# Value pages in two sets of buffers, three orders changed in one attention layer of a decoder step

## The chip, the cores and the metric

One core of one Trainium2 chip runs the whole program in one launch. The metric is the device time of one execution in microseconds (us); lower is better. The kernel before has a median of 2101.49 us over 3 runs (2100.57 to 2105.2).

## The reference

One inference step of a two-layer decoder trunk in float32. 512 prompt tokens and 8 sample tokens (one for each of 8 sequences) go through the same weights. Each layer is a half-step SwiGLU feed-forward, a mixer, a second feed-forward and a gated per-layer embedding, with a norm before and after each. Layer 0's mixer is attention with forget gates beside a gated short convolution; layer 1's is a linear recurrence. The change lies in layer 0's mixer alone:

```
q, k, v, f_lin, b_gate, c_gate, x_in = split(h @ w_in)
logf = log_sigmoid(f_lin + b_f)
# prompt: 8 heads of 64, 512 tokens, blocks of 128 queries
s = q @ k.T * scale + cumsum(logf)[q] - cumsum(logf)[k]; causal mask
y_a = softmax(s) @ v
# sample: 8 sequences, each 256 past rows in 2 pages of 128 rows, plus the new row
k_past, v_past, f_past = cache_k[page_table], cache_v[page_table], cache_logf[page_table]
y_a = softmax(q @ [k_past, k].T * scale + decays) @ [v_past, v]
# both
y_b = b_gate * causal_dwconv(c_gate * x_in)
y = concat(y_a, y_b) @ w_out
```

Keys, values, gates and states come out as further outputs.

## The kernel before

Activations lie feature-major: 128 features on the partitions, 520 tokens (512 + 8) along the row, in 8 chunks of features. Each float32 matrix product is made of three products of reduced precision: high part of the weights by high part of the activations, low by high, high by low. A unit of weights (128 x 2048, 1 MB) is loaded by SP into a slot `raw` (three slots), ScalarE copies out the high part `w_hi` (L690), and VectorE writes the low part `w_lo` over the raw one (L1085). Both are called by `done(name)` at a place that the plan (`make_plan`, `refills`) fixes: the name of a tile stands for the unit that is split there, two units ahead of its use. SP issues the load of a unit when the tile three units earlier is finished.

TensorE takes its work in an order written out by hand, and each engine has its own list; semaphores tie them. `acc_ready` counts finished tiles of TensorE, and `drained` (one count for each of the four PSUM accumulators) counts the emptied ones. `claim` makes TensorE wait until an accumulator is empty.

In `attention` a loop over the 8 heads h runs on TensorE (from L2153): column tiles of the projections (`c`, `x` for heads 0 to 3, `b` for heads 4 to 7, each of 8 chunks of 6 products), `transposes(h)` of the probabilities `sc` into two accumulators (L2133), `scores(h + 1)` (L2095), then the values product `pv` of head h (from L2169). At head 7 the transposes stand inside tile `b3`, after one of its chunks, and `scores` falls away. ScalarE (from L889) copies the transposed probabilities into `pt` in two parts, `pt.0` (key blocks 0 and 1) and `pt.2` (2 and 3), takes the exponentials of head h + 1 (L883), copies out the result of the values product into `q` (L916, L917), and then splits the next unit's high part, where this head has one (heads 0, 1, 2, 3, 5 and 6). VectorE (from L1593) drains the column tiles with `scaled` (L1335), runs the softmax of head h + 1 (L1503 to L1518) and then `w_lo`.

The sample tokens' pages are gathered by GpSimd (`gather`, L590): four pages (`RING`) of 256 KB into the one buffer `ring`, first four steps of keys, then four of values, in an order written into its loop over the heads (from L637), among the rows of decays (`decay_row`) and the copies of q and k to the other partitions (`swap_halves`). A gather waits for the TensorE job that used the ring last. TensorE's products with the keys and values (`key_scores` L2022, `decode_out` L2042) have 2 columns each and stand between chunks of the column tiles: `decode_out(0)` in `x3`, 1 to 3 in `b0`, `b1`, `b2`. `xsum`, `ysum`, `rs_post` and the upper right blocks of `sc` hold nothing that is used between the start of this mixer and its output product.

Of the kernel before, what the change touches and what calls it, by code (L numbers as in the profile page):

```python
# [297 lines left out]
def trunk(nc, weights, params_d, const_d, x_d, p_d, kpages_d, vpages_d, lfpages_d, table_d,  # L298
# [8 lines left out]
    with ctx:  # L307
# [3 lines left out]
        def sem(name):  # L311
            return ctx.enter_context(nc.semaphore(name))
# [115 lines left out]

        def outer(ap, b0=0):

            return ap.rearrange("p (b n) -> p b n", n=P)[:, b0::QB - 1, :]
# [18 lines left out]
        ring_loaded = sem("ring_loaded")  # L450
        lf_loaded = sem("lf_loaded")
# [114 lines left out]
        def _(pool):  # L566
# [12 lines left out]
            for s in range(SUBS):  # L579
# [4 lines left out]
                if s == S_AB:  # L584
# [5 lines left out]
                    def gather(step):  # L590

                        src = kpages_d if step < STEPS else vpages_d
                        at = step % STEPS * RING
                        pages = [pool.value_load(table[0:1, n:n + 1], min_val=0, max_val=kpages_d.shape[0] - 1)
                                 for n in range(at, at + RING)]
                        if step:
                            wait_job(pool, f"{s}.dec_{'so'[(step - 1) // STEPS]}{(step - 1) % STEPS}")
                        for i, page in enumerate(pages):
                            pool.dma_start(ring[:, i, :], src[bass.ds(page, 1), :, :]
                                           .rearrange("a p n -> (a p) n")).then_inc(ring_loaded, 16)  # L600

# [35 lines left out]
                    for h in range(2, HEADS):  # L637
# [7 lines left out]
                        if h != 4:  # L645
                            gather(h + 1 if h < 4 else h)
# [23 lines left out]
        def _(act):  # L670
# [189 lines left out]
            def attention(s):  # L860
# [28 lines left out]
                for h in range(HEADS):  # L889
# [13 lines left out]
                    if h + 1 < HEADS:  # L903
                        exponentials(h + 1)
# [13 lines left out]
                    for n in tiles_at(s, h):  # L918
                        done(n)
# [859 lines left out]
        def _(pe):  # L1779
# [229 lines left out]
            def attention(s):  # L2009
# [32 lines left out]
                def decode_out(i, part):  # L2042

                    if part == 0:
                        claim(J[f"{s}.dec_o{i}"])
                        wait_drained(pe, f"{s}.dec_p")
                        pe.wait_ge(ring_loaded, 16 * RING * (STEPS + i + 1))
# [3 lines left out]
                    for c in range(part % 2 * 2, part % 2 * 2 + 2):  # L2051
                        at = (r // PAGES * AC + c) * 2
                        for g in range(PAGES):
                            src = g * BH + b * HEADS + 2 * c
                            ins = nc.tensor.matmul(a[:, 0, at:at + 2], ring[:, r + g, c * P:(c + 1) * P],  # L2055
# [97 lines left out]
                for h in range(HEADS):  # L2153
# [8 lines left out]
                    for m in B_TILES.get(h, []):  # L2162
                        column_tile(f"b{m}", f"b{m // 2 * 2}", m % 2, with_values(h - 3) if h < MIX_HEAD else
                                    lambda c: transposes(MIX_HEAD) if c == 5 else None)
# [6 lines left out]
                    wait_drained(pe, f"{s}.pt{h}.2")  # L2171
# [3 lines left out]
                    for kb in range(QB):  # L2175
                        values = v_tok[:, kb, h * HD:(h + 1) * HD]
                        if kb < QB - 1:
# [136 lines left out]
```

## Time and profile before

| | |
|---|---|
| median of 3 runs | 2101.49 us (2100.57 to 2105.2) |
| profiled execution | 2097.6 us, of which 2095.9 us span |
| TensorE busy (products) | 2073.0 us (99%) |
| weight loads of TensorE | 2050.4 us (98%) |
| VectorE | 1127.0 us (54%) |
| ScalarE | 703.8 us (34%) |
| mean granted clock of TensorE | 0.997 |

The span is from the first to the last instruction of one execution; the profiled execution is longer by 1.7 us that lie around it. Busy times are shares of the span. PE is TensorE's products, PEld its weight loads, DVE VectorE, ACT ScalarE, POOL GpSimd and SP the engine that issues the weights. The granted clock is a share of the full one: 1.00 is 2.4 GHz, and near 0.5 is 1.2 GHz.

### The profile page before, as it was taken

Reading aid. Unit: us, or ns where it says so; the run is one execution under the profiler, and the core shown is the slowest. Engines: PE = TensorE matmul, PEld = TensorE weight load, DVE = VectorE, ACT = ScalarE, POOL = GpSimd, SP = SyncE. Lnnn points to the kernel's source line nnn. Section 1 sums busy time; section 2 is a strip of 40 time slices with the busy share of each in tenths; the row PEclk is TensorE's granted clock in tenths of the full one; section 3 lists DMA queues with packets and bytes.
Section 4 is the critical chain, followed back from the end, with each engine's and each line's share of the span. In section 5 each row is a group of like instructions: output and inputs, shape, how many; then the busy total and the mean of one; then the engine's idle time right before and its main releaser. Section 6 shows DMA issues by size and latency. Waiting matters only on the chain.

```text
span 2095.9 us, 37938 instructions
## 1 busy us (share of the span) xinstructions
PE 2073.0 (99%) x17092; PEld 2050.4 (98%) x17092; DVE 1127.0 (54%) x1509; ACT 703.8 (34%) x877; POOL 46.5 (2%) x93
## 2 busy tenths in 40 slices
PE   8999999999999999999999999999999999999999
PEld 8999999999889999999999999999999999999998
DVE  6443244856767544234686443244898854323467
ACT  5221123423344422122344221122487432212243
POOL 0000000021210000000000000000000000000000
PEclk9999999999999999999999999999999999999999
DMA  5222222145331322222222222222222222222222
GB/s 175 88 92 88 96 101 81 63 152 142 126 128 61 104 98 91 91 101 81 100 75 101 99 91 94 98 82 81 82 100 84 81 101 101 82 100 83 99 92 82
DMA packets 35075, 202.81 MB, mean 97 GB/s; under 512 B 5056, under 2 KB 5344, under 8 KB 16992
## 3 DMA queue, kind: packets, MB, share of 16 engines
q1 hardware_dynamic: 29520, 183.87, 24.9%
q0 software_dynamic: 5392, 16.50, 2.5%
q8 instruction: 135, 2.21, 0.4%
q14 instruction: 28, 0.23, 0.0%
HBM read 193.78 MB, written 4.48 MB: 95 GB/s over the span
## 4 chain that ended last, share of the span: by engine, by line
PE 86%; DVE 10%; ACT 2%; DMA 2%; issue 1%; DVEq 0%; POOLq 0%; POOL 0%; ACTq 0%
PE acc L1790 70%; PE acc L1900 10%; DVE w_lo L1085 2%; PE acc L1831 1%; DVE t L1198 1%; DMA raw<-in_weights 1%; DVE x L1205 1%; DVE act_lo L1211 1%; DVE rs_post L1193 1%; PE acc L1980 1%; PE acc L2034 1%; DVE xsum L1220 1%; PE acc L2055 1%; DVE rs_pre L1193 0%; PE acc L2104 0%
## 5 line engine op out<-in xcount | busy, mean ns | idle before, releaser
L1790 PE MATMUL acc<-act_hi,w_hi 128*128 128x260 f32 x3072 | 622.1, 284 | 0.0
L1790 PE MATMUL acc<-act_hi,w_lo 128*128 128x260 f32 x3072 | 618.0, 283 | 0.0
L1790 PE MATMUL acc<-act_lo,w_hi 128*128 128x260 f32 x3072 | 617.7, 283 | 0.0
L1790 PEld LDWEIGHTS acc<-act_hi,w_hi 128*128 128x128 f32 x3072 | 472.9, 188 | 2.7 <-issue 2.0
L1790 PEld LDWEIGHTS acc<-act_hi,w_lo 128*128 128x128 f32 x3072 | 472.9, 188 | 0.4
L1790 PEld LDWEIGHTS acc<-act_lo,w_hi 128*128 128x128 f32 x3072 | 472.4, 188 | 0.5
L690 ACT ACTIVATE w_hi<-raw 128x2048 fp32r<-128x2048 f32 (+3 forms) x179 | 323.0, 1805 | 298.2 <-DMA raw<-in_weights 298.0
L1085 DVE TENSOR_TENSOR w_lo<-raw,w_hi 128x2048 fp32r<-128x2048 f32 (+3 forms) x179 | 386.6, 2160 | 38.2 <-ACT w_hi L690 38.1
L1335 DVE TENSOR_TENSOR gu<-acc,rs_pre 128x520 f32<-128x520 f32 x164 | 114.5, 699 | 440.6 <-PE acc L1790 440.4
L816 ACT ACTIVATE hid_hi<-gu 128x520 fp32r<-128x520 f32 x86 | 55.0, 639 | 476.4 <-DVE gu L1355 476.4
L1790 PE MATMUL acc<-hid_hi,w_hi 128*128 128x260 f32 x1024 | 206.3, 283 | 0.2
L1790 PE MATMUL acc<-hid_hi,w_lo 128*128 128x260 f32 x1024 | 206.1, 283 | 0.0
L1790 PE MATMUL acc<-hid_lo,w_hi 128*128 128x260 f32 x1024 | 205.7, 282 | 0.0
L1790 PEld LDWEIGHTS acc<-hid_hi,w_hi 128*128 128x128 f32 x1024 | 157.7, 188 | 1.0 <-DVE hid_lo L1358 1.0
L1790 PEld LDWEIGHTS acc<-hid_lo,w_hi 128*128 128x128 f32 x1024 | 157.7, 188 | 0.0
L1790 PEld LDWEIGHTS acc<-hid_hi,w_lo 128*128 128x128 f32 x1024 | 157.7, 188 | 0.0
L1900 PE MATMUL acc<-act_lo,w_hi 128*128 128x260 f32 x696 | 142.2, 286 | 3.7 <-DVE act_lo L1211 3.6
L1423 DVE COPY y<-acc 128x520 f32<-128x520 f32 x32 | 22.4, 700 | 228.7 <-PE acc L1790 228.7
L1900 PE MATMUL acc<-act_hi,w_hi 128*128 128x260 f32 x696 | 144.0, 288 | 0.0
L1900 PE MATMUL acc<-act_hi,w_lo 128*128 128x260 f32 x696 | 140.1, 283 | 0.0
L812 ACT ACTIVATE gu<-gu 128x520 f32<-128x520 f32 x86 | 54.9, 638 | 217.2 <-DVE gu L1335 217.2
L1900 PEld LDWEIGHTS acc<-act_lo,w_hi 128*128 128x128 f32 x696 | 107.0, 188 | 7.6 <-DVE act_lo L1211 7.3
(295 smaller groups left out, 2139.8 us busy)
## 6 DMA issues: line engine op xcount, KB each, us to landing
raw<-in_weights SPq DMA_DIRECT2D x138, 1024.0 KB, 4.8
raw<-in_weights SPq DMA_DIRECT2D x32, 896.0 KB, 4.5
ring<-in_k_pages POOLq DMA_DIRECT2D x16, 256.0 KB, 4.0
ring<-in_v_pages POOLq DMA_DIRECT2D x16, 256.0 KB, 3.7
raw<-in_weights SPq DMA_DIRECT2D x12, 256.0 KB, 5.2
x<-in_x SPq DMA_DIRECT2D x8, 260.0 KB, 6.5
out_y<-x SPq DMA_DIRECT2D x8, 260.0 KB, 2.5
ckb<-ch_rows POOLq DMA_DIRECT2D x8, 256.0 KB, 4.3
```

The source lines that it names most:

```text
L690: nc.scalar.activation(w_hi[n % SLOTS][:, at:size], raw(n, size)[:, at:size], ACT.Copy)\
L812: nc.scalar.activation(g, g, ACT.Silu).then_inc(silu_ready, 1)
L816: nc.scalar.activation(hid_hi[:, j if j < HID[0] else j - HID[0], :], up, ACT.Copy).then_inc(hidh_ready, 1)
L1085: nc.vector.tensor_tensor(w_lo[n % SLOTS][:, at:size], raw(n, size)[:, at:size], w_hi[n % SLOTS][:, at:size].bitcast(F32), ALU.subtract).t ...
L1193: nc.vector.reciprocal(cols(rs, half), cols(rs, half)).then_inc(rs_ready, 1)
L1198: nc.vector.scalar_tensor_tensor(out=cols(t[c % 2], half), in0=cols(y[:, c, :], half), scalar=post_gain(s, c), in1=cols(rs_post, half), op ...
L1205: nc.vector.tensor_tensor(cols(x[:, c, :], half), cols(x[:, c, :], half), cols(t[c % 2], half), ALU.add)\
L1211: nc.vector.scalar_tensor_tensor(out=cols(act_lo[:, c, :], half), in0=cols(x[:, c, :], half), scalar=pre_gain(s, c), in1=cols(act_hi[:, c, ...
L1335: drains(nc.vector.tensor_tensor(two(out), tile_of(J[name]), two(rs_pre[:, :]), ALU.mult), name)
L1423: drains(nc.vector.tensor_copy(two(y[:, m, :]), tile_of(J[name])), name)
L1790: ins = nc.tensor.matmul(a[0:width, half, 0:HALF], w[slot][:, at:at + width], m[:, half * HALF:(half + 1) * HALF], start=first and n == 0, ...
L1900: ins = nc.tensor.matmul(accs[:, n, 0:HALF], w[unit % SLOTS][:, at:at + P], part, start=c == 0 and k == 0, stop=c == KC - 1 and k == 2)
```

## The change

Values are gathered into two sets of buffers in turn: steps 0 and 2 into `ring`, steps 1 and 3 into `xsum`, `ysum`, `rs_post` and the unused blocks of `sc` (the fourth page in two transfers, 384 and 128 columns). The gather of step 1 waits for no product and is issued at head 2, that of step 2 at head 4 behind `dec_o0`, and that of step 3 at head 5 behind `dec_o1`. ScalarE splits a head's high part after the copies to `pt` and ahead of the next head's exponentials. The values product waits for `pt.0` at its start and for `pt.2` only before key block 2. The transposes of head 7 stand after chunk 6 of `b3`, not after chunk 5.

```diff
--- before.py
+++ after.py
@@ -426,6 +426,16 @@
         def acc_of(name):
             return acc[PLAN.acc[J[name]]]
 
+        def spare_page(r, c):
+
+            if r < RING - 1:
+                return (xsum, ysum, rs_post)[r][:, c * P:(c + 1) * P]
+            return sc[:, 0, (c + 1) * P:(c + 2) * P] if c < AC - 1 else sc[:, 1, 2 * P:3 * P]
+
+        def value_page(i, r, c):
+
+            return spare_page(r, c) if i % 2 else ring[:, r, c * P:(c + 1) * P]
+
         def outer(ap, b0=0):
 
             return ap.rearrange("p (b n) -> p b n", n=P)[:, b0::QB - 1, :]
@@ -448,6 +458,7 @@
         half_hi, half_lo = sem("half_hi"), sem("half_lo")
         p_loaded = sem("p_loaded")
         ring_loaded = sem("ring_loaded")
+        spare_loaded = sem("spare_loaded")
         lf_loaded = sem("lf_loaded")
         hi_ready, lo_ready = sem("hi_ready"), sem("lo_ready")
         acc_ready = sem("acc_ready")
@@ -594,10 +605,26 @@
                         pages = [pool.value_load(table[0:1, n:n + 1], min_val=0, max_val=kpages_d.shape[0] - 1)
                                  for n in range(at, at + RING)]
                         if step:
-                            wait_job(pool, f"{s}.dec_{'so'[(step - 1) // STEPS]}{(step - 1) % STEPS}")
+                            before = step - 2 if step > STEPS else step - 1
+                            wait_job(pool, f"{s}.dec_{'so'[before // STEPS]}{before % STEPS}")
                         for i, page in enumerate(pages):
                             pool.dma_start(ring[:, i, :], src[bass.ds(page, 1), :, :]
                                            .rearrange("a p n -> (a p) n")).then_inc(ring_loaded, 16)
+
+                    def gather_spare(step):
+
+                        at = step % STEPS * RING
+                        pages = [pool.value_load(table[0:1, n:n + 1], min_val=0, max_val=kpages_d.shape[0] - 1)
+                                 for n in range(at, at + RING)]
+                        if step > STEPS + 1:
+                            wait_job(pool, f"{s}.dec_o{step - STEPS - 2}")
+                        for i, page in enumerate(pages):
+                            whole = vpages_d[bass.ds(page, 1), :, :].rearrange("a p n -> (a p) n")
+                            if i < RING - 1:
+                                pool.dma_start((xsum, ysum, rs_post)[i][:, 0:D_A], whole).then_inc(spare_loaded, 16)
+                            else:
+                                pool.dma_start(sc[:, 0, P:SEQ], whole[:, 0:D_A - P]).then_inc(spare_loaded, 16)
+                                pool.dma_start(sc[:, 1, 2 * P:3 * P], whole[:, D_A - P:D_A]).then_inc(spare_loaded, 16)
 
                     gather(0)
                     for n in range(DEC * PAGES):
@@ -642,8 +669,14 @@
                             wait_drained(pool, f"{s}.k{c}")
                             wait_first(pool, s, c)
                             swap_halves(c)
-                        if h != 4:
-                            gather(h + 1 if h < 4 else h)
+                        if h < 4:
+                            gather(h + 1)
+                        if h == 2:
+                            gather_spare(STEPS + 1)
+                        if h == 4:
+                            gather(STEPS + 2)
+                        if h == 5:
+                            gather_spare(STEPS + 3)
                     wait_drained(pool, f"{s}.k3")
                     store(k_o, k[:, :, :])
                     wait_drained(pool, f"{s}.v3")
@@ -901,6 +934,8 @@
                         drains(nc.scalar.activation(pt[:, kb + 1, (kb + 1) * P:SEQ], a[:, 1, (kb + 1) * P:SEQ], ACT.Copy),
                                name)
                     if h + 1 < HEADS:
+                        for n in tiles_at(s, h):
+                            done(n)
                         exponentials(h + 1)
                     if h == MIX_HEAD:
 
@@ -915,8 +950,8 @@
                     a, out = acc_of(name), q[r:r + HD, h // 2, 0:SEQ]
                     chained(nc.scalar.activation(outer(out), outer(a[0:HD, 0, :]), ACT.Copy))
                     drains(nc.scalar.activation(out[:, P:3 * P], a[HD:P, 0, P:3 * P], ACT.Copy), name)
-                    for n in tiles_at(s, h):
-                        done(n)
+                for n in tiles_at(s, MIX_HEAD):
+                    done(n)
                 for i in range(STEPS):
                     wait_drained(act, f"{s}.dec_o{i}")
                 for c in range(AC):
@@ -2044,7 +2079,10 @@
                     if part == 0:
                         claim(J[f"{s}.dec_o{i}"])
                         wait_drained(pe, f"{s}.dec_p")
-                        pe.wait_ge(ring_loaded, 16 * RING * (STEPS + i + 1))
+                        if i % 2:
+                            pe.wait_ge(spare_loaded, 16 * (RING + 1) * (i // 2 + 1))
+                        else:
+                            pe.wait_ge(ring_loaded, 16 * RING * (STEPS + i // 2 + 1))
                     a = acc_of(f"{s}.dec_o{i}")
                     r = part // 2 * PAGES
                     b = (i * RING + r) // PAGES
@@ -2052,7 +2090,7 @@
                         at = (r // PAGES * AC + c) * 2
                         for g in range(PAGES):
                             src = g * BH + b * HEADS + 2 * c
-                            ins = nc.tensor.matmul(a[:, 0, at:at + 2], ring[:, r + g, c * P:(c + 1) * P],
+                            ins = nc.tensor.matmul(a[:, 0, at:at + 2], value_page(i, r + g, c),
                                                    pT[:, src:src + 2], start=g == 0, stop=g == PAGES - 1)
                     if part == 3:
                         ins.then_inc(acc_ready, 1)
@@ -2161,19 +2199,20 @@
                                     (lambda c: decode_scores() if c == 2 else None) if h == 2 else None)
                     for m in B_TILES.get(h, []):
                         column_tile(f"b{m}", f"b{m // 2 * 2}", m % 2, with_values(h - 3) if h < MIX_HEAD else
-                                    lambda c: transposes(MIX_HEAD) if c == 5 else None)
+                                    lambda c: transposes(MIX_HEAD) if c == 6 else None)
                     if h < MIX_HEAD:
                         transposes(h)
                     if h + 1 < HEADS:
                         scores(h + 1)
                     a = claim(J[f"{s}.pv{h}"])
                     wait_drained(pe, f"{s}.pt{h}.0")
-                    wait_drained(pe, f"{s}.pt{h}.2")
                     if h == 0:
                         wait_drained(pe, f"{s}.vt0")
                         wait_drained(pe, f"{s}.vt2")
                     for kb in range(QB):
                         values = v_tok[:, kb, h * HD:(h + 1) * HD]
+                        if kb == 2:
+                            wait_drained(pe, f"{s}.pt{h}.2")
                         if kb < QB - 1:
                             inner = slice(max(kb, 1) * P, (QB - 1) * P)
                             nc.tensor.matmul(a[HD:P, 0, inner], values, pt[:, kb, inner],
```

## Rows read from the trace of the kernel before

**Rows 1.** The page's first part: busy time and share of the span.
```profile
PE 2073.0 (99%) x17092; PEld 2050.4 (98%) x17092; DVE 1127.0 (54%) x1509; ACT 703.8 (34%) x877; POOL 46.5 (2%) x93
```
**Rows 2.** Waits in the attention, 470 to 625: waiter, releaser: total us, times, longest.
```profile
PEld acc L2179 <- ACT pt L901: 5.3, 6, 0.9
...
PE acc L2104 <- DVE t L1335: 1.8, 1, 1.8
```
**Rows 3.** Timeline of TensorE: start, length, instruction. Values product of heads 1, 4.
```profile
512.88 0.59 PE L2104 MATMUL acc<-xsq 64*128 64x512 f32 x1
513.53 0.40 PE L2179 MATMUL acc<-pt,v_tok 128*64 128x256 f32 x1
...
570.70 0.59 PE L2104 MATMUL acc<-ysq 64*128 64x512 f32 x1
571.22 0.43 PE L2179 MATMUL acc<-pt,v_tok 128*64 128x256 f32 x1
```
**Rows 4.** Timeline of ScalarE, copies to pt of head 1.
```profile
512.32 0.49 ACT L901 ACTIVATE pt<-acc 128x384 f32<-128x384 f32 x1
...
513.11 0.28 ACT L901 ACTIVATE pt<-acc 128x128 f32<-128x128 f32 x1
```
**Rows 5.** Timeline of ScalarE, head 3.
```profile
555.29 0.28 ACT L901 ACTIVATE pt<-acc 128x128 f32<-128x128 f32 x1
558.37 0.40 ACT L883 ACTIVATE sc<-sc,nmx 128x128 f32<-128x128 f32 x1 [2.80 <-DVE nmx L1512]
...
564.34 1.92 ACT L690 ACTIVATE w_hi<-raw 128x2048 fp32r<-128x2048 f32 x1
```
**Rows 6.** Timeline of VectorE, end of head 3.
```profile
563.75 1.27 DVE L1518 TENSOR_SCALAR sc<-sc,rden 128x128 f32<-128x128 f32 x4
566.28 2.29 DVE L1085 TENSOR_TENSOR w_lo<-raw,w_hi 128x2048 fp32r<-128x2048 f32 x1 [1.26 <-ACT w_hi L690]
```
**Rows 7.** Timeline of GpSimd: issues in the second half of the attention.
```profile
581.19 2.29 POOL L599 DMA_DIRECT2D ring<-in_v_pages x4 [4.58 <-PE acc L2055]
583.48 0.54 POOL L575 DMA_DIRECT2D out_k<-k x1
```
**Rows 8.** Timeline of TensorE, value parts of steps 2 and 3.
```profile
575.46 1.84 PE L2055 MATMUL acc<-pT,ring 128*128 128x2 f32 x16
...
578.70 1.84 PE L2055 MATMUL acc<-pT,ring 128*128 128x2 f32 x16
...
590.58 2.20 PE L2055 MATMUL acc<-pT,ring 128*128 128x2 f32 x16 [1.47 <-DMA ring<-in_v_pages]
...
595.38 1.78 PE L2055 MATMUL acc<-pT,ring 128*128 128x2 f32 x15
```
**Rows 9.** Windows: length, busy us of PE, PEld, DVE, ACT, POOL, granted clock, DMA share, GB/s.
```profile
523.50:526.70 3.20, 3.20 (x17) 3.18 (x17) 2.56 (x4) 0.57 (x1) 2.16 (x4) 0.55 0.35 99
...
566.70:569.60 2.90, 1.25 (x12) 1.01 (x10) 2.81 (x4) 1.64 (x4) 1.45 (x3) 1.00 0.79 261
...
592.60:595.90 3.30, 3.30 (x18) 3.30 (x19) 2.29 (x1) 0.17 (x1) 0.00 (x0) 0.56 0.57 233
```
**Rows 10.** Timeline of ScalarE, heads 6 and 7.
```profile
601.06 0.28 ACT L901 ACTIVATE pt<-acc 128x128 f32<-128x128 f32 x1
601.63 0.40 ACT L883 ACTIVATE sc<-sc,nmx 128x128 f32<-128x128 f32 x1 [0.29 <-DVE nmx L1512]
...
605.94 0.72 ACT L883 ACTIVATE sc<-sc,nmx 128x512 f32<-128x512 f32 x1 [0.99 <-DVE nmx L1512]
```
**Rows 11.** Timeline of TensorE, head 7 to the output product.
```profile
608.33 1.31 PE L2140 MATMUL acc<-const,sc 128*128 128x128 f32 x10 [1.05 <-DVE sc L1518]
609.40 0.49 PE L1790 MATMUL acc<-act_hi,w_hi 128*128 128x260 f32 x2
...
612.44 0.75 PE L1980 MATMUL acc<-act_hi,w_hi 128*128 128x260 f32 x4
```
**Rows 12.** Loads of weights into raw, 540 to 620: us from issue to landing.
```profile
DMA to landing us min/median/max: 4.9/5.9/7.7
```

## Prediction

> **What bounds the kernel now.** I read the page's busy shares first. TensorE's products fill 99% of the span, its weight loads 98%; the next engine, VectorE, has 54% [rows 1]. So only what TensorE waits for, or runs at a lower clock, can be won, and that is little: 2095.9 - 2073.0 = 22.9 us of idle in the whole span. Next the waits, for the attention alone [rows 2], then the timelines of TensorE, ScalarE, VectorE and GpSimd there, and last the granted clock by stretches. The reader is to see four losses that the edits touch: a small gap ahead of most values products, one wait of 1.8 us ahead of a score product, one of 1.47 us for value pages with a stretch of low clock behind it, and one of 1.05 us ahead of the last transposes. All else in this layer's mixer is dense.
>
> **Part by part.**
>
> *Values wait by halves.* The weight loads' row promises 5.3 us in six waits [rows 2], but a weight load stands idle while the last score products still stream, and TensorE loses only the gap in its own starts. At head 1 the first value product starts 513.53 - 512.88 = 0.65 us after the last score product; at head 4, where pt was long ready, 571.22 - 570.70 = 0.52 [rows 3]. Heads 1, 2, 3, 5 and 6 lie within 0.01 of head 1, so 0.13 each is the wait. The bounds are 0 (a second wait with the same gap) and 5.3/6 = 0.9 each; I take 0.13, the measured difference in starts. With the change, pt.0 has been copied at 512.32 + 0.49 = 512.81 and pt.2 at 513.11 + 0.28 = 513.39 [rows 4], both ahead of the last score product's end (512.88 + 0.59 = 513.47), so no new wait forms at key block 2. At heads 0, 1, 2 and 5 nothing is late behind it: 4 x 0.13 = 0.5 us. At heads 3 and 6 a chain of VectorE decides what follows, so TensorE only arrives earlier at the next wait: 0.
>
> *High parts ahead of the exponentials.* At head 3 the split of the next unit ran behind the exponentials and the copies of the result, at 564.34 for 1.92 us [rows 5]. VectorE, free at 563.75 + 1.27 = 565.02, waited 1.26 us for it and did the low part until 568.57 [rows 6]. Only then came the drain of tile b0, and TensorE, which needs that accumulator for the scores, stood 1.8 us [rows 2]. After the change the split runs in ScalarE's gap between 555.29 + 0.28 = 555.57 and 558.37, which is 2.80 us long [rows 5]: it costs nothing there and VectorE starts the low part at once. So the drain comes 1.26 us earlier, and 1.8 - 1.26 = 0.5 us of the wait stays (0.65 as TensorE comes 0.13 earlier). The bounds are 0 and 1.8; I take 1.26, VectorE's own row. At heads 0 to 2 TensorE had no such wait, so nothing is won there. At heads 5 and 6 the gap before the first exponential is only 0.29 us [rows 10]. But the fourth exponential waits for VectorE's maximum until 605.94 in any case: from 601.06 + 0.28 = 601.34 that is 4.6 us, which hold the split (1.9) and three exponentials that are each shorter than the fourth (under 0.72, together under 2.2). The softmax ends as before: 0. Without that cover it would cost 1.6 us at head 6 and none at head 5, whose transposes come far later. A split waits for its weights in ScalarE's list, with exponentials and copies queued behind; loads land 4.9 to 7.7 us after issue [rows 12] and are issued more than that ahead of the new places (the nearest, head 6's, is weighed below).
>
> *Two sets of value buffers.* The last step's gather could start only when step 2 had left the ring: its issues began at 581.19 [rows 7], and TensorE waited 1.47 us for them at 590.58 [rows 8]. With two sets it goes out behind step 1, so before step 2 begins at 575.46 [rows 8], at least 6 us earlier and ahead of the stores of k and v (583.48, [rows 7]) with which it shared the queues; it is there before 590.58 - 1.47 = 589.1 even at the landing time of before (590.58 less 581.19 + 2.29, 7.1 us). On GpSimd 14 transfers in place of 12 bring the second to fourth step, all of them moved. At head 2 five issues of about 0.55 us and four page numbers are put ahead of `decay_row(3)` and `swap_halves(2)`, at head 4 a gather that waits for `dec_o0` ahead of `decay_row(5)` and `swap_halves(3)`: these come up to 13 us later, at about 555 to 557, for scores that TensorE reaches at 583. The stores move from 583 to about 577. Nothing is late by that: 0. The gain is 1.47 us and what the wait drew behind it.
>
> *The clock behind that wait.* Between the two value parts of step 2 lie 578.70 - 575.46 = 3.24 us, of step 3 595.38 - 590.58 = 4.80 us [rows 8]. The granted clock from 592.6 to 595.9 was 0.56, so near 1.2 GHz [rows 9], and nothing is waited for in that stretch. I count the 4.80 - 3.24 = 1.56 us as gained with the wait. Its bounds are 0 and 1.56 from above, and from below -1.56, a new stretch of this kind elsewhere: the stretch from 523.5 to 526.7 had 0.55 with no wait before it, only the thin products with the keys, and the wait before 569.7 left the clock at 1.00 [rows 9]. The Trainium skill (TensorE: Matmul & The Clock Gate, "The HAM clock gate") says that low clock is the default state which activity lifts, and that the check runs free of the kernel's start. By that rule the same program has such a stretch in some executions and not in others; the rows above agree with it, and it is a rival below.
>
> *Last transposes a chunk later.* From the scores of head 7 to its probabilities VectorE's chain is fixed; the transposes start at 608.33 as seen from those scores, whatever TensorE does in between [rows 11]. So chunk 6 (0.73 us) fills the wait of 1.05, and some 0.45 (with head 6's 0.13) stays. Behind them only chunk 7 is left: 609.40 + 0.73 = 610.13. ScalarE begins its copies 0.97 us after the transposes, as at head 1 (609.30), has pt.0 after 1.12 (610.42) and pt.2 after 1.70 (611.00), and TensorE starts 0.14 us behind pt.0, at 610.56. It has done two key blocks at 611.0, waits for pt.2 until 611.14, and needs 0.78 more: 611.92, against 612.44 [rows 11]. Gain 0.52; the bounds are 0 and the whole 1.05.
>
> *Sum.* 0.5 + 1.26 + 1.47 + 1.56 + 0.52 = 5.3 us. The profiled execution took 2097.6 us (span 2095.9 and 1.7 around it), so 2092.3. The median of the runs shown, 2101.5, lies 3.9 above it; the savings are waits in the same list of work, so I carry the difference over: **2096.2 us**. All later work is TensorE's, so it moves up as a whole.
>
> **The rivals.**
>
> *The low clock stays or turns up elsewhere.* For it: thin products alone were enough at 523.5. Against: of the three earlier value steps none was followed by it. Price: the 1.56 falls away, gain 3.8, time 2097.7. If in turn the stretch at 523.5 goes too, the gain is 6.9 and the time 2094.6.
>
> *The waits are handed on.* Heads 3 and 6 show how: a gap that is closed makes TensorE earlier at a wait that VectorE sets. If the split brings nothing at head 3 (the drain turns out bound by something else), and head 7's gain is lost at the output product's first wait for `act_lo`, then 0.5 + 1.47 + 1.56 = 3.5 remain: 2098.0.
>
> *The pages are no earlier.* The change doesn't do what it says if GpSimd comes late to the third gather because `decay_row` holds its list. Then 1.47 and 1.56 fall away, gain 2.3, time 2099.2. Against: the row of decays before it waits for a softmax that is over.
>
> *Slower: ScalarE stands for weights at head 6.* Its split now stands ahead of the exponentials. The load for it is issued when b1 ends, two chunks behind the release of the gather at 581.19 [rows 7], so near 582, and is to be there when head 6's copies end, 601.3 [rows 10] less the 3.0 us won ahead of it, 598; in the case before, such loads took up to 7.7 us [rows 12]. The stores of 2.1 MB now lie just before it. If it landed more than 16 us after issue, each further us would move the exponentials, the transposes and the output product by as much (less some 0.8 of slack); beyond 22 us the kernel is slower than before. At 26 us it would be 2101.5 - 5.3 + 9.2 = 2105.4. Against it: three times the longest landing seen.
>
> **How the numbers follow.** My chances are 0.50 for the forecast (own range 2094.7 to 2097.7), 0.20 for the low clock that stays, 0.08 for both stretches gone, 0.12 for handed-on waits, 0.06 for pages no earlier, 0.04 for slower. The runs shown spread over 4.6 us, so the range is 2092.0 to 2100.6: from the forecast less the untouched stretch and some spread to past the pages' case. A measurement of this kernel tells about 0.2%, 4.2 us, from no change, so the border is 2097.3. Below it lie most of the forecast's case (0.44), the 0.08 and some of the low-clock case (0.08): 0.60 faster, 0.36 within, 0.04 slower.
>
> **What would show it.** Right: no wait of a value product for pages; `w_hi` at heads 0 to 6 straight behind the copies to pt, and no wait of `w_lo` for it; the wait for tile b0's drain at 0.4 to 0.8 us; the last transposes' at 0.3 to 0.7; the first value product 0.5 us behind the last score product; clock 1.00 behind step 3. Wrong: a wait of ScalarE for weights in this mixer, a wait of the scores for swapped halves, or a third stretch near 1.2 GHz.

## The result: faster by 0.55%, twice what was forecast

| | before | changed |
|---|---|---|
| median of the runs, us | 2102.37 (2100.57 to 2105.2, 4 runs) | 2090.84 (2089.15 to 2091.75, 4 runs) |
| profiled execution, us | 2097.6 | 2091.75 |
| its span, us; mean granted clock | 2095.9; 0.997 | 2089.9; 0.999 |

The ratio is 0.9945, with an interval of 0.993 to 0.996: 11.5 us less, and 2090.84 lies below the forecast range (2092.0 to 2100.6). The spans of the two profiled executions differ by 6.0 us, close to the forecast sum of 5.3. The attention alone, from the first key product to the output product, takes 606.18 - 454.10 = 152.1 us where it took 612.44 - 454.57 = 157.9, so 5.8 less. So the list of savings fits the two traces; what does not fit is the step from the trace to the median.

The page's first part of the changed kernel (busy us, share of the span, instructions; before in [rows 1]): products and weight loads are each about 4 us shorter in sum, with the same count.

```profile
PE 2068.6 (99%) x17092; PEld 2046.3 (98%) x17092; DVE 1125.9 (54%) x1509; ACT 702.9 (34%) x877; POOL 47.7 (2%) x95
```

The waits of the changed kernel from 465 to 620 us (waiter, releaser: total us, times, longest), to be held beside [rows 2]. No row says that a value product waits for pages. The wait for tile b0's drain (the scores', L2142) is 0.9 where it was 1.8; the last transposes' (L2178) is 0.5 where it was 1.05; a new small one of 0.2 stands ahead of the last values. The one row of `w_lo` waiting for `w_hi` is that of the unit behind head 7 (at 612.4); at heads 0 to 6 there is none.

```profile
PEld acc L2218 <- ACT pt L934: 4.5, 6, 0.8
...
PE acc L2142 <- DVE t L1370: 0.9, 1, 0.9
DVE w_lo L1120 <- ACT w_hi L723: 0.9, 1, 0.9
...
PE acc L2178 <- DVE sc L1553: 0.5, 1, 0.5
PE acc L2218 <- ACT pt L934: 0.2, 1, 0.2
```

ScalarE's timeline in the changed kernel, head 3 and head 6 (start, length, instruction, idle before and its releaser; before in [rows 5] and [rows 10]). The split `w_hi` now stands straight behind the copies to pt. At head 6 the fourth exponential is still released by VectorE, 0.99 us after ScalarE was free, just as before: the split delayed nothing.

```profile
554.34 0.28 ACT L934 ACTIVATE pt<-acc 128x128 f32<-128x128 f32 x1
554.51 1.91 ACT L723 ACTIVATE w_hi<-raw 128x2048 fp32r<-128x2048 f32 x1
557.44 0.40 ACT L916 ACTIVATE sc<-sc,nmx 128x128 f32<-128x128 f32 x1 [1.02 <-DVE nmx L1547]
...
595.38 0.28 ACT L934 ACTIVATE pt<-acc 128x128 f32<-128x128 f32 x1
595.56 1.90 ACT L723 ACTIVATE w_hi<-raw 128x2048 fp32r<-128x2048 f32 x1
597.36 0.40 ACT L916 ACTIVATE sc<-sc,nmx 128x128 f32<-128x128 f32 x1
...
600.26 0.72 ACT L916 ACTIVATE sc<-sc,nmx 128x512 f32<-128x512 f32 x1 [0.99 <-DVE nmx L1547]
```

VectorE's timeline in the changed kernel, end of head 3 (before in [rows 6]): the low part `w_lo` starts right behind the scaling, where it had waited 1.26 us, and only then comes b0's drain (L1370).

```profile
562.81 1.27 DVE L1553 TENSOR_SCALAR sc<-sc,rden 128x128 f32<-128x128 f32 x4
564.00 2.28 DVE L1120 TENSOR_TENSOR w_lo<-raw,w_hi 128x2048 fp32r<-128x2048 f32 x1
566.20 0.36 DVE L1621 TENSOR_TENSOR q<-acc,onew 64x8 f32<-64x8 f32 x2
566.59 0.70 DVE L1370 TENSOR_TENSOR t<-acc,rs_pre 128x520 f32<-128x520 f32 x1
```

GpSimd's timeline in the changed kernel: the last step's pages are asked for from 564.57 on, 22.0 us before TensorE uses the first of them at 586.53 (before: from 581.19, 9.4 us ahead of their first use at 590.58 [rows 7, 8]); the stores follow from 574.30.

```profile
564.57 0.57 POOL L624 DMA_DIRECT2D xsum<-in_v_pages  x1 [8.49 <-PE acc L2093]
...
574.30 0.54 POOL L586 DMA_DIRECT2D out_k<-k  x1
```

TensorE's timeline in the changed kernel: the wait for b0's drain, a values product (head 5), the last step's two value parts, and head 7 (before in [rows 3], [rows 8] and [rows 11]). The first value product starts 582.33 - 581.80 = 0.53 us behind the last score product (0.65 at this head before). The two value parts begin 3.22 us apart (4.80 before). From the last transposes to the output product it is 606.18 - 602.65 = 3.53 us (4.11 before).

```profile
567.43 0.34 PE L2142 MATMUL acc<-k,q 64*128 64x128 f32 x1 [0.89 <-DVE t L1370]
...
581.80 0.59 PE L2142 MATMUL acc<-xsq 64*128 64x512 f32 x1
582.33 0.43 PE L2218 MATMUL acc<-pt,v_tok 128*64 128x256 f32 x1
...
586.53 0.28 PE L2093 MATMUL acc<-pT,xsum 128*128 128x2 f32 x2
...
589.75 0.28 PE L2093 MATMUL acc<-pT,rs_post 128*128 128x2 f32 x2
...
602.65 1.31 PE L2178 MATMUL acc<-const,sc 128*128 128x128 f32 x10 [0.46 <-DVE sc L1553]
...
604.94 0.40 PE L2218 MATMUL acc<-pt,v_tok 128*64 128x256 f32 x1 [0.25 <-ACT pt L934]
...
606.18 0.74 PE L2015 MATMUL acc<-act_hi,w_hi 128*128 128x260 f32 x4
```

Windows of the changed kernel (length, busy us of PE, PEld, DVE, ACT, POOL, granted clock, DMA share, GB/s). At the last step's second value part the clock is 1.00 (0.56 before [rows 9]). The stretch near 1.2 GHz at 523.5 is still in this execution.

```profile
523.50:526.70 3.20, 3.20 (x17) 3.20 (x17) 2.75 (x7) 0.00 (x0) 2.71 (x5) 0.53 0.56 172
589.70:593.00 3.30, 3.30 (x31) 3.30 (x31) 2.08 (x3) 0.00 (x0) 0.00 (x0) 1.00 0.00 0
```

**Where the other half comes from.** Each execution lists its span and its mean granted clock; their product is about the span that it would have had at full clock. (Low clock in the last us of the span, behind TensorE's last product, counts as a loss here and costs nothing: 1.0 us in the trace of before, nearly 0 in that of the changed kernel.) The clock has three digits, 1 us in the product of a single execution, so only means are used. Fifty-two executions of the kernel before, from the first two sets of runs below, have a mean span of 2099.2 us and a product of 2091.0: 8.2 us go to low clock. Their spans follow the clock, from 2095.5 on average where it was 0.998 to 2102.1 where it was 0.994. Nine executions of the changed kernel have 2088.7 and 2085.9: 2.8 us. So the mean span fell by 10.5 us: 5.1 at full clock and 5.4 by low clock that is no longer there. The trace from which the forecast was made had a span of 2095.9, one of the short ones. Its clock of 0.997 makes some 6.3 us of low clock, of which the sum held 1.56.

Where these stretches lie is read from the clock records of the profiles, each a single execution. Between 470 and 625 us low clock costs 3.4, 1.7, 5.1 and 6.8 us in the four profiles with one ring and pages waited for (before, e1_before, e1_orders_alone, e2_stores_late), and 0 or 1.7, on average 0.7, in the seven with two sets and no such wait. Elsewhere, near 1600 us and behind the last product, both have it: 0.1 to 2.8 and 0 to 2.8 us. So most of the difference lies in this mixer, but not all low clock does.

### The profile page after: what moved, and what is told of

Same layout as the page of the kernel before. It is cut to its first block, busy times and chain, and to the rows that moved or that the text cites. A ratio compares the mean times of both kernels' runs of the same rounds, so it can differ in the third digit from the quotient of the medians.

```text
span 2089.9 us, 37944 instructions
## 1 busy us (share of the span) xinstructions
PE 2068.6 (99%) x17092; PEld 2046.3 (98%) x17092; DVE 1125.9 (54%) x1509; ACT 702.9 (34%) x877; POOL 47.7 (2%) x95
## 4 chain that ended last, share of the span: by engine, by line
PE 86%; DVE 11%; ACT 2%; issue 1%; DMA 1%; DVEq 0%; ACTq 0%
PE acc L1825 70%; PE acc L1935 10%; DVE w_lo L1120 2%; DVE t L1233 2%; PE acc L1866 1%; DVE x L1240 1%; DVE act_lo L1246 1%; DMA raw<-in_weights 1%; DVE rs_post L1228 1%; PE acc L2015 1%; PE acc L2069 1%; DVE xsum L1255 1%; DVE rs_pre L1228 0%; PE acc L2093 0%; PE acc L2142 0%
## 5 line engine op out<-in xcount | busy, mean ns | idle before, releaser
L1370 DVE TENSOR_TENSOR gu<-acc,rs_pre 128x520 f32<-128x520 f32 x164 | 114.3, 698 | 441.1 <-PE acc L1825 441.0
```

The costliest lines, as they stand in the source:

```text
L1370: drains(nc.vector.tensor_tensor(two(out), tile_of(J[name]), two(rs_pre[:, :]), ALU.mult), name)
```

## The experiments

Two questions. Which part carries the gain, the two sets of buffers or the three orders? And does the low clock follow the waits for pages, or does it come by itself?

**e1_before: the kernel before, unchanged**, for executions and a second profile of it.

> The kernel before, unchanged, for a second profile of it and more times. Its profiled execution took 2097.6 us, its timed ones 2100.6 to 2105.2, so 3 to 7.6 us more; the changed kernel's profiled and timed ones agree within 2.6 us. Theory A (the wait for the last value pages and the low clock behind it are longer in most executions than in the one that was profiled): this profile, if its execution takes over 2100 us, shows more than the 1.47 + 1.56 us there, some 6 to 10 us. Theory B (the extra time lies outside this layer's mixer, in stretches of low clock or waits that the change doesn't touch): the mixer's loss stays at 3 us and the extra shows elsewhere. Theory C (the chip on which before was first timed differs): the times are near 2097.

Measured: 2100.51 us (11 runs, 2097.33 to 2105.21), ratio 0.9999 (0.9989 to 1.0009). TensorE's timeline in its profile shows two waits for pages, the first of them at step 1, where the trace that I predicted from has none. It is from the same code; so which gathers come too late differs by execution. The profiled execution took 2097.44 us, again a quick one, so theory A's condition (over 2100) isn't met and no execution of the usual length has been profiled. The wait at step 1 also cost little in the end: the scores' wait for b0's drain is 0.20 us here, where it was 1.8, and the attention takes 611.35 - 454.62 = 156.7 us, 1.1 less than in the trace of the forecast, with 1.7 less of low clock in it. The clock stays at 1.00 behind this first wait (the window below); behind the second it falls.

```profile
560.45 1.92 PE L2055 MATMUL acc<-pT,ring 128*128 128x2 f32 x16 [1.60 <-DMA ring<-in_v_pages]
...
568.46 0.34 PE L2104 MATMUL acc<-k,q 64*128 64x128 f32 x1 [0.20 <-DVE t L1335]
...
589.50 2.02 PE L2055 MATMUL acc<-pT,ring 128*128 128x2 f32 x16 [1.65 <-DMA ring<-in_v_pages]
```

```profile
561.20:564.60 3.40, 3.40 (x32) 3.40 (x31) 1.64 (x6) 3.10 (x5) 0.54 (x1) 1.00 0.24 77
```

**e1_after: the changed kernel, unchanged.**

> The changed kernel, unchanged, timed in five rounds beside before. A and B: near 2090.8, ratio to before 0.993 to 0.996. C: ratio near 0.997, the 6.0 us by which the two profiled spans differ (2095.9 and 2089.9).

Measured: 2090.62 us (5 runs, 2088.88 to 2090.99), ratio 0.995 (0.9937 to 0.9963). The gain holds in a second set of runs. In its profile the stretch of the thin products with the keys has full clock, in the window's columns as above:

```profile
523.40:526.80 3.40, 3.40 (x31) 3.36 (x30) 3.37 (x6) 0.00 (x0) 1.57 (x3) 1.00 0.11 23
```

In e1_before too the clock is 1.00 there. So the stretch at 523.5 is not a fixture of the code, with or without the change.

**e1_sets_alone: the two sets, without the three orders.** The changed kernel with the three orders put back (main lines; the split behind `MIX_HEAD` returns into the loop as well):

```diff
-                        for n in tiles_at(s, h):
-                            done(n)
                         exponentials(h + 1)
...
+                    for n in tiles_at(s, h):
+                        done(n)
...
-                                    lambda c: transposes(MIX_HEAD) if c == 6 else None)
+                                    lambda c: transposes(MIX_HEAD) if c == 5 else None)
...
+                    wait_drained(pe, f"{s}.pt{h}.2")
...
-                        if kb == 2:
-                            wait_drained(pe, f"{s}.pt{h}.2")
```

> Before with the two sets of value buffers alone; the three orders are as before. My forecast's terms give 1.47 + 1.56 = 3.0 us, and theories B and C say the same: 3.0 us faster than before in the times. Theory A: about 3.0 plus the 5.5 us that the forecast missed, so 8 to 9 us faster in the times. The trace shows no wait of the value products in any case.

Measured: 2092.7 us (5 runs, 2092.31 to 2094.57), ratio 0.9965 (0.9952 to 0.9978). So 8.0 of the 10.1 us that the whole change brought beside it come from the two sets, although the untouched waits stay: the profile's waits have 2.1 us for b0's drain and 1.0 for the last transposes.

```profile
PE acc L2140 <- DVE t L1368: 2.1, 1, 2.1
...
PE acc L2176 <- DVE sc L1551: 1.0, 1, 1.0
```

Mean clock 0.9988, as in the changed kernel: the low clock goes with the sets. By the means, the sets alone bring 2.1 us at full clock (2088.9 against 2091.0) and 5.7 of low clock; the three orders on top of them bring 3.0 at full clock (2085.9).

**e1_orders_alone: the three orders, with the one ring of before.** The kernel before with the same lines moved the other way.

> The changed kernel with one ring, as before: only the split ahead of the exponentials, the wait by halves and the later transposes. My terms give 0.5 + 1.26 + 0.52 = 2.3 us, and theory A says 2 to 3 us faster than before, with the page wait still there and as long as before or longer by the 2 us that TensorE comes earlier (then the gain is lost at that wait, and about 0 to 1 is left). Theories B and C: 2 to 3 as well; if instead it is 7 to 8 us faster, the missed 5.5 us belong to the orders and A falls.

Measured: 2098.83 us (12 runs, 2094.97 to 2108.21), ratio 0.9997 (0.9985 to 1.0009). At full clock the mean span is 2.0 us shorter than before (2089.0 against 2091.0; forecast for these three 2.28), but 9.1 us are lost to low clock where before lost 8.2. So the orders win what was forecast at full clock, and the times, which spread over 13 us, don't tell it. Its two waits for pages are 3.4 us in sum, in e1_before 3.2: that the gain comes back as a longer wait is not shown. TensorE's timeline, then the windows behind the first of the two waits, and the one behind the second (1.9 us), where the clock is 1.00:

```profile
560.20 1.92 PE L2057 MATMUL acc<-pT,ring 128*128 128x2 f32 x16 [1.50 <-DMA ring<-in_v_pages]
```

```profile
561.20:564.60 3.40, 3.40 (x26) 3.40 (x25) 2.48 (x7) 1.57 (x4) 0.54 (x1) 0.77 0.25 77
564.60:568.00 3.40, 3.40 (x17) 3.40 (x18) 1.70 (x3) 0.00 (x0) 0.06 (x1) 0.50 0.00 0
568.00:571.40 3.40, 3.40 (x18) 3.40 (x18) 1.23 (x2) 0.00 (x0) 2.09 (x4) 0.50 0.62 196
571.40:574.80 3.40, 3.40 (x19) 2.07 (x20) 1.48 (x5) 1.98 (x6) 0.00 (x0) 0.73 0.35 112
...
595.20:598.60 3.40, 3.40 (x32) 3.40 (x31) 1.45 (x1) 0.00 (x0) 0.00 (x0) 1.00 0.70 285
```

The reader is to see that TensorE is busy in all of the first four (3.40 of 3.40), with 17 and 18 products in the two at 0.50, where the last one holds 32 at full clock: nothing waits there, it is only slow. A list of waits does not show this loss; the clock column does.

**e2_stores_late: is it the stores that delay the gathers?** The kernel before, with the stores of k, v and the states held until tile b3:

```diff
+                    wait_job(pool, f"{s}.b3")
                     wait_drained(pool, f"{s}.k3")
```

> The kernel before with one ring and its old orders; only the stores of k, v, the gates and the convolution's state (2.1 MB) are held back until tile b3 is finished. Theory A1 (the wait for the last pages, and the low clock that it draws, come from the pages sharing the queues with the stores): the pages land in about 4 us in place of 7, the wait behind them is gone, and most of what two sets of buffers gave (8.0 us) is here too: 2093 to 2096, with a narrow spread. Theory A2 (one ring is too late by itself; the executions differ in how long the pages of any step take, stores or not): little changes at step 2, the spread stays wide and the time lies within 2 us of before, near 2099 to 2101.

Measured: 2098.31 us (11 runs, 2091.99 to 2101.97), ratio 0.9982 (0.9972 to 0.9993). In its profile two waits for pages of 1.9 us in sum are left, the longer 1.6, at step 1. The last step's is 0.3 us, and low clock stands behind it all the same (the windows):

```profile
PE acc L2056 <- DMA ring<-in_v_pages: 1.9, 2, 1.6
```

```profile
592.00:595.40 3.40, 3.40 (x24) 3.40 (x24) 2.13 (x3) 1.80 (x1) 0.00 (x0) 0.74 0.00 0
595.40:598.80 3.40, 3.40 (x17) 3.40 (x17) 1.06 (x3) 0.00 (x0) 0.00 (x0) 0.50 0.00 0
```

So in this profile sharing with the stores makes most of the last step's wait, and by the medians some 2.4 us of the time (1.5 to 5.9 by the interval), where the sets bring 8.0. The result lies between the two theories; the rest comes with the earlier start of the gathers.

**e2_no_split, e2_no_halves, e2_no_late: the changed kernel with one of the three orders put back** (each with its lines of the diff under e1_sets_alone).

> The changed kernel with the split of the high parts back behind the exponentials. My term for it is 1.26 us, so near 2091.9 where the changed kernel has 2090.7; the wait of the scores for tile b0's drain is about 2.0 us in place of 0.9. If the edit brings nothing in the end, 2090.7; if more hangs on it (low clock behind that wait), 2093 or more.

> The changed kernel with the values product waiting for both copies at its start again. My term is 0.5 us: near 2091.2; the start of the first value product 0.65 us behind the last score product in place of 0.52. The weight loads' row (4.5 us in six waits) would give 2095.

> The changed kernel with the last transposes back behind chunk 5. My term is 0.5 us for the place of the transposes and the shorter wait together, so 2090.9 to 2091.3; the wait of the transposes for the probabilities is about 1.2 us in place of 0.5. If the wait counts in full, 2091.4.

| put back | median, us (runs) | ratio (interval) | forecast for it |
|---|---|---|---|
| the split behind the exponentials | 2094.92 (6) | 0.9969 (0.9957 to 0.9981) | +1.26 |
| values wait for both copies | 2090.56 (5) | 0.995 (0.9938 to 0.9963) | +0.5 |
| last transposes a chunk earlier | 2092.9 (6) | 0.9953 (0.9941 to 0.9964) | +0.52 |

Without the split ahead it is 4.1 us longer than the changed kernel's 2090.84, over three times the term. TensorE's timeline has the wait for b0's drain back:

```profile
568.46 0.34 PE L2140 MATMUL acc<-k,q 64*128 64x128 f32 x1 [2.26 <-DVE t L1368]
```

That is 1.37 more than the 0.89 of the changed kernel, 0.11 above the forecast term. The windows behind it have clocks of 0.68 (568.0 to 571.4) and 0.82 (571.4 to 574.8), together some 3.40 x 0.32 + 3.40 x 0.18 = 1.7 us. But the means don't show low clock as the cause: it is 2.8 us in this kernel as in the changed one, and 4.4 us lie at full clock (2090.3 against 2085.9), of which the trace has 1.37. The rest is not resolved. One wait in another layer, in its output product (1605 to 1611 us), has 0.7 or 2.2 us from one execution to the next, in the kernel before and in the changed one (two profiles each). Nor do the parts add up: with all three orders put back (e1_sets_alone) the median is 2092.7, 2.2 below this one, though the intervals overlap (0.9952 to 0.9978 and 0.9957 to 0.9981). Without the halves the gap is back in the trace, 581.50 - 580.85 = 0.65 us, but the times don't show it. Without the later transposes their wait is 1.2 us in the trace; the runs spread from 2089.4 to 2095.48, so its 2 us are not told from the forecast 0.5. So the worth of the three orders is measured as a whole (2.1 us by the medians, 3.0 by the means at full clock, forecast 2.28), and of the single ones only the split's stands out.

**e3_filled: more work in place of idle.** The kernel before, with twelve products that nothing reads ahead of the waits for pages at steps 1 and 3 (2.9 us more of TensorE's work):

```diff
                         wait_drained(pe, f"{s}.dec_p")
+                        if i % 2:
+                            slot = U[f"{s}.b{i - 1}"] % SLOTS
+                            for at in range(12):
+                                nc.tensor.matmul(acc_of(f"{s}.dec_o{i}")[:, 1, 0:HALF], w_hi[slot][:, at * P:(at + 1) * P],
+                                                 act_hi[:, 0, 0:HALF], start=True, stop=True)
                         pe.wait_ge(ring_loaded, 16 * RING * (STEPS + i + 1))
```

> The kernel before with 12 idle products (128 x 260, about 0.12 us each, 1.44 us together; their result is never read) put in front of the waits for the value pages of steps 1 and 3, where three of four profiles of one-ring kernels show waits of 1.5 to 1.9 us. The waits for data stay as long; TensorE is only not idle in them. Theory I (low clock follows from TensorE standing idle among thin products): the mean granted clock rises from 0.996 to about 0.998 and the time falls by 2 to 4 us against before, to 2097 to 2099, though TensorE has 2.9 us more work. Theory T (the thin products alone bring it about, or the low stretches have nothing to do with the pages): the clock stays at 0.996 and the time is 2100 to 2102.

Measured: 2095.45 us (12 runs, 2092.21 to 2104.08) against 2099.93 beside it, ratio 0.9981 (0.9968 to 0.9993): with more work it is faster, by 4.5 us of the medians, a little more than the 2 to 4 of theory I. Nothing in the edit asks for the pages earlier; only TensorE is not idle meanwhile. In the profile, of a quick execution (2092.53), no wait for pages is left and no low clock stands in the attention. By the means the gain is low clock: 4.4 us where before in the same set has 7.4 (mean clock 0.9979 and 0.9965), and at full clock nearly nothing (2090.5 and 2091.1). That speaks for the low clock as a consequence of the idle time. A rival stays: the products are also more work among the thin ones, and it may be that, and not the wait that they fill, which keeps the clock up.

**e3_last_late: a wait put back.** The changed kernel, its last gather held until step 2 is done:

```diff
-                            wait_job(pool, f"{s}.dec_o{step - STEPS - 2}")
+                            wait_job(pool, f"{s}.dec_o{step - STEPS - 1}")
...
-                        if h == 5:
+                        if h == 7:
                             gather_spare(STEPS + 3)
```

> The changed kernel with two sets, but the last step's gather issued at head 7 behind step 2, as one ring would do it. Theory I: TensorE waits for these pages alone, 1.5 to 3 us, and the clock falls behind that in a part of the executions: 2093 to 2096, clock 0.997 to 0.998, spread wider than the changed kernel's. If the whole loss of before were the plain wait, 2092.2 to 2093; if step 1 alone were to blame, 2091.

Measured: 2096.74 us (11 runs, 2090.65 to 2099.89), ratio 0.9981 (0.9968 to 0.9994): 5.9 us above the changed kernel, and 0.7 above theory I's range. TensorE's timeline and the windows behind it:

```profile
588.06 0.35 PE L2093 MATMUL acc<-pT,xsum 128*128 128x2 f32 x2 [1.82 <-DMA sc<-in_v_pages]
```

```profile
588.40:591.80 3.40, 3.40 (x25) 3.40 (x25) 2.59 (x2) 0.00 (x0) 0.00 (x0) 0.76 0.98 407
591.80:595.20 3.40, 3.40 (x19) 3.40 (x17) 0.00 (x0) 0.00 (x0) 0.00 (x0) 0.50 0.03 10
595.20:598.60 3.40, 3.40 (x17) 3.40 (x17) 0.38 (x3) 0.00 (x0) 0.00 (x0) 0.50 0.00 0
598.60:602.00 3.40, 3.40 (x18) 2.35 (x16) 2.00 (x5) 1.90 (x5) 0.00 (x0) 0.73 0.00 0
```

One wait of 1.82 us, then four windows that hold 3.40 x (0.24 + 0.50 + 0.50 + 0.27) = 5.1 us less of the clock. At 0.50 that is a stretch of 10.2 us near 1.2 GHz; the first and the last window are at full clock in part. This is one execution. By the means of 11, low clock takes 4.6 us, 1.8 more than in the changed kernel and hardly clear of noise, and 3.5 lie at full clock (2089.3 against 2085.9), more than the wait; that part is not resolved. The Trainium skill (TensorE: Matmul & The Clock Gate, "HAM oscillation — how this bites in real kernels") describes this for a matmul whose tiles are short beside its DMA waits: the wait lets the clock fall, and the next tile starts slow. The trace agrees, with 0.50 behind a wait of 1.82 us amid thin products.

Over all 13 profiles, each with four steps of values, TensorE waits for pages at 8 steps of 52, for 0.3 to 1.9 us. Behind 6 of the 8 waits the clock falls within about 3 us; behind the wait at step 1 in e1_before (1.60) and that at the last step in e1_orders_alone (1.9) it stays at 1.00, and behind the 44 steps without a wait it never falls in that time (the stretch in e2_no_split follows the wait for b0's drain). So the low clock there goes with the wait for pages, but not with every one, and not by its length alone.

**e3_low_later: the wait that is left.** The changed kernel, where at head 3 VectorE makes the low part behind b0's drain:

```diff
                         scaled(t[m % 2][:, :], f"{s}.b{m}")
+                        if h == AC:
+                            for n in tiles_at(s, h - 1):
+                                done(n)
...
-                    for n in tiles_at(s, h):
+                    for n in tiles_at(s, h) if h != AC - 1 else []:
```

> An improvement on the changed kernel: at head 3 VectorE makes the next unit's low part only behind the drain of b0, for which TensorE waits 0.9 us there. Expected 2089.8 where the changed kernel has 2090.7, no wait of the scores for that drain; a little more (2089.3) if low clock followed that wait in some executions.

Measured: 2089.41 us (6 runs, 2087.55 to 2090.36), ratio 0.9945 (0.9931 to 0.9959). In its profile the scores wait for no drain any more. It is the shortest median of all, 1.4 below the changed kernel's. But its ratio to before is 0.9945, as the changed kernel's was in its first runs (0.995 in the second), and the kernel before was 0.8 us quicker in this set of runs (2099.93) than in that of e1_after: the gain is not shown.

## Why the prediction was right in kind and wrong in size

- *Values wait by halves*: the starts lie 0.53 us apart, forecast 0.52. (Head 0, which the sum counts with the others, had 0.73 and not 0.65.) Right in the trace; e2_no_halves shows that the times don't tell it.
- *High parts ahead*: ScalarE's gap took the split, `w_lo` waits no more at heads 0 to 6. The scores' wait is 0.89 where I said 0.5 to 0.65, and outside the band of 0.4 to 0.8 by a tenth. The term won 0.9 between the two traces (1.8 to 0.89), but in e2_no_split the same wait is 2.26: the waits for pages taken away, TensorE is at b0 earlier (in e1_before, which waits 1.60 at step 1, the scores wait only 0.2). As a wait its worth in the changed kernel is thus 1.37 (forecast 1.26); by the times it is 4.1, and what makes the rest stays open.
- *Two sets*: the last gather went out 16.6 us earlier (564.57 against 581.19) where I wrote at least 6 (5.7 by the rows). The pages were there, as forecast, and nothing on GpSimd or in the scores came late by it. The sets alone bring 2.1 us at full clock, where the row had one wait of 1.47; the second profile of the same kernel has waits of 1.60 and 1.65, at two steps.
- *The clock behind that wait*: 1.00, as forecast, where it was 0.56. (The row that I named for the clock behind the wait at 569.7 ends before that wait does; the trace has 1.00 behind it too.) The size is wrong. The term was 1.56 with bounds from -1.56 to 1.56; by the means, low clock fell by 5.4 in the whole kernel, and by 5.7 with the sets alone.
- *Last transposes a chunk later*: wait 0.46 (forecast 0.45), transposes to output product 3.53 us where it was 4.11, so 0.58 (forecast 0.52).
- *Rivals*: the low clock did not stay, and no wait was handed on beyond those priced. Head 6's split delayed the fourth exponential by nothing, so the slower case did not occur. That the stretch at 523.5 comes and goes was part of the rule of the Trainium skill that I cited. Rows of one execution could not bear it out, as I wrote they did; the runs do (0.53 in one profile of the changed kernel, 1.00 in the other).

**The step that failed** stands in the term for the clock and in the *Sum*: "the savings are waits in the same list of work, so I carry the difference over". The low clock was priced at one stretch of one execution, and the 3.9 us between that execution and the median were taken as a constant that has nothing to do with the change. They were not: the profiled execution (2097.6) was quicker than all three timed ones (2100.57 to 2105.2), and what it lacked was in part more low clock (6.3 us by its clock, 8.2 in the mean), a loss that two sets of buffers remove. In the means low clock falls by 5.4 us, where the sum has 1.56. At full clock they fall by 5.1, where the sum has 3.75 of waits: the mechanism was right, the waits nearly so in size, and the remaining 1.35 is not accounted for. The wait at step 1 can't be shown to be it: in the one profile that sets it beside mine (e1_before), b0's drain gives back 1.6 us of it. The two parts make the 10.5 us of the means. Had I taken the profiled execution's savings as the least and the 3.9 as partly curable, the forecast would have lain between 2092.3 and 2096.2: nearer, and still above 2090.84.

What was only argued: that the 5.4 us of low clock all follow waits for pages. The sets alone take them away (mean clock 0.9988), 6 of the 8 waits in the profiles have low clock behind them, and e3_filled raises the mean clock without moving a gather. But e3_last_late lowers it in the means by little more than noise, no execution of the usual 2100 us has been profiled, and a stretch such as that at 523.5, which has no wait before it, also occurs; the changed kernel still loses 2.8 us to it and its like. Open stays why such a stretch lasts 3.4 us in one place and 10.2 in another, why two of the waits have none, and the rest of e2_no_split's 4.1.

## What to carry to other kernels

Before a term is sized, hold the profiled execution's own time against the timed runs: where it is the quickest, part of the missing time can be losses that its rows don't show and that the change removes. A wait of one execution can also be another's gain elsewhere (e1_before), so compare the whole stretch and not the row alone. Span times mean clock, over many executions, parts roughly what is waited for from what is run slowly. On a TensorE that is 99% busy, price a wait amid thin products with the clock that may follow it (here behind 6 of 8), in a column that no list of waits contains.

## What the hardware showed that I had not expected

- A wait of 1.82 us was followed by 10.2 us near half clock in one execution, and the edit that made the wait made the kernel 5.9 us longer by the medians (e3_last_late). Waits of 1.60 and 1.9 us elsewhere left the clock at 1.00.
- Twelve products that nothing reads, put ahead of each of two waits, made the kernel 4.5 us faster though they are 2.9 us of work (e3_filled).
- Two executions of one kernel differ in which gather lands late: 1.47 us at step 3 alone in one profile, 1.60 at step 1 and 1.65 at step 3 in the other.
